# A fused mixer and mixture-of-experts layer in float32: the modulation's products move to VectorE, the first row norm is reordered, and eight unread products go

## What is computed

```python
def first_block(x, ...):
    hn = rmsnorm(x, norm_g)                       # the first row norm
    z = jnp.einsum('bsd,de->bse', hn, w_in)       # 1024 x 4252 weights, then split
    # attention in a band of chunks, an mLSTM and a gated linear attention (GLA) read pieces of z
    y = jnp.concatenate([y_a, y_b, y_c], axis=-1)
    return rmsnorm(x + jnp.einsum('bse,ed->bsd', y, w_out), final_g)

def second_block(x, c, ...):
    c_act = jax.nn.silu(c)
    mod = c_act @ ada_w[i] + ada_b[i]             # the modulation: 1024 x 6144 weights, one row
    sh1, sc1, gt1, sh2, sc2, gt2 = split(mod, 6)
    # a latent attention, an RWKV-7 recurrence, then 32 experts of width 1024, 4 for each token
```

## Time and profile before

| | |
|---|---|
| median of three runs | 1948.76 us |
| the profiled execution, its own time | 1948.07 us |
| its span in the trace | 1946.4 us |
| TensorE busy | 1865.2 us, 96% |
| VectorE busy | 1618.8 us, 83% |
| ScalarE busy | 1165.2 us, 60% |
| GpSimd busy | 366.1 us, 19% |
| TensorE's mean granted clock | 0.983 of full speed |

### The profile page before, as it was taken

The page is one execution under the profiler, slowest core; times in us unless marked ns, Lnnn a source line. Parts: engine busy times, 40 slices in busy tenths (PEclk is TensorE's granted clock), DMA queues, the critical chain, the costliest instruction groups (busy, mean ns, idle before and its releaser), DMA issues.

```text
span 1946.4 us, 27313 instructions
## 1 busy us (share of the span) xinstructions
PE 1865.2 (96%) x9416; PEld 1514.7 (78%) x9416; DVE 1618.8 (83%) x1719; ACT 1165.2 (60%) x1179; POOL 366.1 (19%) x356
## 2 busy tenths in 40 slices
PE   7999989999999888999999999999999999999997
PEld 6767767776677777888888888888888888888884
DVE  5776777954578487899999999999999999999996
ACT  5543344324462521577777777777777777777773
POOL 3431110020071710611101111111111111111110
PEclk9999999999998998999999999999999999999999
DMA  7535534232001143999999999999999999999994
GB/s 207 174 103 180 193 117 181 85 99 65 11 1 34 34 177 113 332 329 398 399 389 398 389 398 393 388 391 383 396 395 383 396 384 387 398 386 398 388 367 153
DMA packets 176818, 525.12 MB, mean 270 GB/s; under 512 B 30754, under 2 KB 48242, under 8 KB 176754
## 3 DMA queue, kind: packets, MB, share of 16 engines
q1 hardware_dynamic: 152722, 457.48, 61.8%
q0 software_dynamic: 21952, 66.78, 11.9%
q10 hardware_dynamic: 2080, 0.01, 0.1%
HBM read 499.08 MB, written 25.15 MB: 269 GB/s over the span
## 4 chain that ended last, share of the span: by engine, by line
PE 58%; DVE 2%; issue 0%; POOLq 0%; POOL 0%; DVEq 0%
PE banks L3625 54%; PE banks L3613 3%; PE banks L3619 1%; PE banks L3693 0%; DVE expert_weights L3973 0%; DVE x_tokens L3969 0%; DVE weights_lo L3764 0%; PE banks L3714 0%; DVE x_tokens L3980 0%; DVE x_tokens L3852 0%; PE banks L3751 0%; PE banks L3684 0%; DVE rows_lo L3794 0%; DVE member L3832 0%; DVE route_work L3874 0%
## 5 line engine op out<-in xcount | busy, mean ns | idle before, releaser
L3764 DVE TENSOR_TENSOR weights_lo<-expert_weights,weights_hi 128x2048 fp32r<-128x2048 f32 x384 | 876.0, 2288 | 66.0 <-ACT weights_hi L4011 62.8
L4011 ACT ACTIVATE weights_hi<-expert_weights 128x2048 fp32r<-128x2048 f32 x384 | 738.8, 1926 | 263.7 <-PE banks L3625 238.8
L3625 PE MATMUL banks<-weights_hi,rows_hi 128*128 128x512 f32 x1024 | 319.1, 393 | 0.0
L3625 PE MATMUL banks<-weights_hi,rows_lo 128*128 128x512 f32 x1024 | 315.5, 389 | 0.0
L3625 PE MATMUL banks<-weights_lo,rows_hi 128*128 128x512 f32 x1024 | 273.8, 389 | 0.0
L3625 PEld LDWEIGHTS banks<-weights_hi,rows_hi 128*128 128x128 f32 x1024 | 189.7, 188 | 44.9 <-issue 7.3
L3625 PEld LDWEIGHTS banks<-weights_hi,rows_lo 128*128 128x128 f32 x1024 | 192.2, 188 | 40.5
L3625 PEld LDWEIGHTS banks<-weights_lo,rows_hi 128*128 128x128 f32 x1024 | 192.2, 188 | 40.0
L3625 PE MATMUL banks<-weights_hi,u_hi 128*128 128x512 f32 x512 | 161.0, 396 | 0.0
L3625 PE MATMUL banks<-weights_hi,u_lo 128*128 128x512 f32 x512 | 157.9, 390 | 0.0
L3625 PE MATMUL banks<-weights_lo,u_hi 128*128 128x512 f32 x512 | 136.9, 389 | 0.0
(11 more groups left out here) (624 smaller groups left out, 2751.1 us busy)
## 6 DMA issues: line engine op xcount, KB each, us to landing
expert_weights<-in_exp_w SPq DMA_DIRECT2D x384, 1024.0 KB, 10.5
enter_rows<-in_ada_w POOLq DMA_DIRECT2D x24, 1024.0 KB, 6.9
w_in_landing<-in_w_in SPq DMA_DIRECT2D x16, 384.0 KB, 3.4
second_landing<-in_w_in SPq DMA_DIRECT2D x12, 512.0 KB, 3.7
x_tokens<-in_x SPq DMA_DIRECT2D x8, 512.0 KB, 7.1
w_in_landing<-in_w_in SPq DMA_DIRECT2D x8, 512.0 KB, 3.7
rwkv_room<-in_w_o SPq DMA_DIRECT2D x8, 512.0 KB, 7.8
w_in_landing<-in_w_in SPq DMA_DIRECT2D x12, 256.0 KB, 4.1
```

Source lines behind the costliest of these rows:

```text
L3625: last = nc.tensor.matmul(c.banks[:, bank + n, :], left[:, 2 * q + kk, :], right[:, q, kk * FF + n * 512:kk * FF + (n + 1) * 512], start=s ...
L3764: nc.vector.tensor_tensor(w_lo[:, ch % SPLIT, :], c.raw[:, ch % RAW if place is None else place, :], w_hi[:, ch % SPLIT, :], ALU.subtract) ...
L4011: nc.scalar.activation(w_hi[:, ch % SPLIT, :], c.raw[:, ch % RAW if place is None else place, :], ACT.Copy).then_inc(hi_ready.sem, 1)
```

## The change

It does five things.

1. `LATE` goes: `add_part` on VectorE does the products and sums of all 24 halves. `scale_half` (ScalarE) and `add_half` (GpSimd) go, eight calls of each. The 32 new operations of VectorE stand at `m` = 6 to 9, 14 to 17, 22 to 25, 30 to 33, 37 to 40, 47 to 50, 54 to 57 and 62 to 65. None stands at 41 to 46.
2. `load_half(i)` waits for VectorE's part of half `i - 2` instead of GpSimd's.
3. The first load of the modulation's weights waits until the last tile of `x` has landed.
4. The row norm: VectorE squares tile 2 before it inverts tile 1's root, and tile 3 before tile 2's. The last tile is normalised by VectorE instead of ScalarE. TensorE starts piece 0 with two low feature parts ready instead of four, and waits for the third and fourth ahead of its banks 2 and 3.
5. The eight unread products ahead of the first sum go.

```diff
-    LATE = 8
+    gate_chain = range(gates_at + 9, gates_at + 15)
     part_at, at_m = {}, 0
     for m, i in sorted(half_at.items()):
-        for kk in range(4 if i >= LATE else 0):
-            at_m = max(at_m + 1, m)
+        for kk in range(4):
+            at_m = max(at_m + 1, m - 1 if i == 4 else m)
+            if at_m in gate_chain:
+                at_m = gate_chain.stop
             part_at[at_m] = (i, kk)
...
-                    if i >= LATE + 2:
-                        pool.wait_ge(part_added.sem, 4 * (i - 1 - LATE))
-                    elif i >= 2:
-                        pool.wait_ge(half_added.sem, i - 1)
+                    if i >= 2:
+                        pool.wait_ge(part_added.sem, 4 * (i - 1))
...
+                pool.wait_ge(x_in[TT - 1].sem, 16)
                 load_half(0)
...
-                        pe.wait_ge(hn_lo.sem, max(2 * q + 2, TT if q == 0 else 0))
+                        pe.wait_ge(hn_lo.sem, 2 * q + 2)
+                    if g == 0 and q == 0 and b >= 2:
+                        pe.wait_ge(hn_lo.sem, b + 1)
...
                 def add_partitions(q):
                     own_last_bank(row_done, q + 1)
-                    if q == 0:
-                        idle(c.banks[:, 7, :], 8)
-                    if 2 * q < LATE:
-                        pe.wait_ge(half_added.sem, 2 * q + 2)
-                    else:
-                        pe.wait_ge(part_added.sem, 4 * (2 * q + 2 - LATE))
+                    pe.wait_ge(part_added.sem, 4 * (2 * q + 2))
...
-                for t in range(TT):
+                def root(t):
                     act.wait_ge(squares.sem, t + 1)
                     nc.scalar.activation(stat[:, 1, t:t + 1], stat[:, 0, t:t + 1], ACT.Sqrt).then_inc(roots.sem, 1)
+                root(0)
+                for t in range(TT - 1):
+                    if t >= 1:
+                        root(t + 1)
                     act.wait_ge(inverses.sem, t + 1)
                     nc.scalar.activation(y[:, t, :], c.x[:, t, :], ACT.Copy, scale=stat[:, 1, t:t + 1]).then_inc(normed.sem, 1)
+                    if t == 0:
+                        root(1)
...
+                square(0)
+                invert(0)
+                square(1)
+                for t in range(2, TT):
+                    square(t)
+                    invert(t - 1)
+                invert(TT - 1)
+                dve.wait_ge(inverses.sem, TT)
+                v.tensor_scalar(y[:, TT - 1, :], c.x[:, TT - 1, :], stat[:, 1, TT - 1:TT], None, ALU.mult).then_inc(last_normed.sem, 1)
                 low(0)
```

More of the change, by code:

```diff
@@ L673, in _ @@
                         mask_corner(i - 19)
-                    if i - 1 < LATE:
-                        add_half(i - 1)
                     if i % 2 == 0 and i >= 4:
@@ L954, in silu_last @@
                     nc.scalar.activation(tok_e[:, b, :], c.banks[:, b, :], ACT.Silu).then_inc(gates_made.sem, 1)
-                def scale_half(i):
-                    q, half = divmod(i, 2)
-                    act.wait_ge(w_in[half].sem, 16 * (q + 1))
-                    if i == 0:
-                        act.wait_ge(c_ready.sem, 1)
-                    for kk in range(4):
-                        k = 4 * half + kk
-                        last = nc.scalar.activation(w_m[:, half, kk, :], w_m[:, half, kk, :], ACT.Copy, scale=c_col[:, k:k + 1])
-                    last.then_inc(half_scaled.sem, 1)
                 def logs():
```

48 lines of the change are left out of this document (17 added, 31 removed).

## The result

The changed kernel took **1931.53 us** in the median of six runs (1928.59 to 1939.87) against 1950.18 us of the kernel before in the same series (six runs): a ratio of **0.9909 [0.9887, 0.9932]**. The forecast was 1943.0 us with a range of 1937 to 1951, so the time lies outside the range, and the move is three times the forecast one. The profiled execution of the changed kernel is the slowest of its six, 1939.87 us (span 1938.0 us), so its early stages are to be read, and not its end. The move of the medians, 18.7 us, is known to about 4 us by the interval.

The account below looks back on a forecast made before the run. TensorE, busy 96% of the span, was taken as the bound, with its waits and low clock. The terms -2.8 + 1.7 - 2.7 - 3.0 + 2.0 - 1.0 gave -5.8 us: 1943.0 us against the median, range 1937 to 1951.

Parts of the forecast that it names:

- the first sum: Mixers' first modulation sum: starts at 47.0 us behind VectorE's eighth operation instead of 49.79, -2.8 us.
- a fall of the clock behind it: Behind the first sum: TensorE idle about 3 us, then 3.4 us at half rate, +1.7 us (0 to +3.0).
- first sum to columns: Ahead of the turned gate columns: VectorE's chain ends earlier and TensorE's wait goes, -2.7 us.
- low clock behind the columns: Behind the turned gate columns: the low clock goes with the wait, -3.0 us (0 if the chain is not shortened).
- the third sum: At m = 51: a new wait for VectorE's half 5 operations, +2.0 us, between 0 and +3.5.
- the GLA's wait and the one at L755: In the GLA: the 1.0 us wait behind slow VectorE operations goes, -1.0 us, between -1.0 and +1.
- the row norm: At the start: piece 0 begins 1.3 to 1.9 us earlier, but spent at the first sum; 0, otherwise 3.6.
- The low part of piece 4: Ahead of the first sum: without GpSimd it ends near 35.3 us instead of 36.50, 1.2 us earlier.
- rival A: At the first sum: the clock does not fall, 1.7 us not paid; 1941.3 us, or 1939; chance 0.30.
- speak against this change: First sum: the skill's clock gate text taken as a sign that removing unread products lets the clock fall.
- VectorE's load: Between 30 and 142 us: 23.8 us added at most, some 15 us back from slow operations, about 9 us net.
- rival D: Later clock falls, as near 253 us, may come or go, 1.7 to 3 us either way; no chance given.

Follow-up runs that it names:

- e3: The kernel before with VectorE making products and sums of all 24 halves; old norm, early load and eight unread products stay: 1938.42 us, ratio 0.9959.
- e1: The changed kernel with the modulation's first load early again, not waiting for the last tile of x: 1936.27 us, ratio 0.9945.
- e2: The changed kernel with the old row norm order and piece 0 waiting for four low parts: 1931.90 us, ratio 0.9932.
- e7: The kernel before without the eight unread products ahead of the first sum: 1947.07 us, ratio 0.9994.
- e8: The kernel before with the new order of the row norm alone: 1947.17 us, ratio 0.9994.
- e5: The changed kernel with the eight unread products put back ahead of the first sum: 1940.43 us, ratio 0.9943.
- e6: The changed kernel without the 11, 4 and 7 unread products ahead of gate columns, keys and first GLA scores: 1932.84 us, ratio 0.9929.
- e11: The changed kernel with 76 more unread products at the head of the latent attention, shifting later stages back: 1949.73 us, ratio 1.0005.
- e9: The changed kernel itself run once more, with nothing changed: 1932.46 us, ratio 0.9916.
- e4: The kernel before with only the modulation's first load waiting for the last tile of x: 1948.69 us, ratio 1.0015.
- e10: The changed kernel without the 4 and 7 unread products ahead of keys and GLA scores, the columns' 11 kept: 1932.09 us, ratio 0.9913.
- e12: The changed kernel with VectorE's modulation operations allowed inside the gate chain, quarters 41 to 46: 1931.02 us, ratio 0.9911.

## Why the prediction was wrong

The prediction's terms beside the trace, up to the end of the mixers (us):

| step | predicted | measured |
|---|---|---|
| the first sum | -2.8 | -5.8 |
| a fall of the clock behind it | +1.7 | 0 |
| first sum to columns | -2.7 | -4.8 |
| low clock behind the columns | -3.0 | -3.1 |
| the third sum | +2.0 | +0.6 |
| the GLA's wait and the one at L755 | -1.0 | -1.6 |
| behind the GLA | not counted | -2.3 |
| sum | -5.8 | -16.9 |

The fourth to sixth rows split the window from the columns to the GLA (-4.0 us) by its busy time and its waits, within 0.1 us.

**The step that failed** is "It starts when VectorE has done its eighth operation ... The sum starts at 47.0 instead of 49.79 ... TensorE ... is idle for about 3 us ahead of it", and with it the row norm's "both are spent at the first sum, where something else is last; the term is 0". The low part of piece 4 was sized well: forecast to end at 35.3, measured 34.98 with the VectorE part alone (e3). From there the prediction took the 9.0 us that the load of piece 6 had needed before; it needed at most 7.6 us (35.0 to 42.58), and why it was shorter stays open. The eighth operation ended at 45.2. That is 1.2 us ahead of TensorE even with the old start. The late load and the norm together brought the same operation to 43.54 (45.72 without the late load in e1, 46.40 without the norm in e2). TensorE stayed last, and three things that the prediction had weighed against one another paid together: the start with its clock (-2.5: 1.0 of start, 1.5 of clock), the eight products (-2.0) and the wait (-1.3). They make the 5.8. These 4.7 us at the first sum and behind it are the largest part of the 11.1 us between forecast and trace. An estimate over a chain of five links was used as if it were good to 1 us; between "VectorE last by 3 us" and "TensorE last by 0.4 us" lay those 4.7 us, and rival A was written as a smaller gap, not as no gap at all.

**The fall behind the first sum** was priced rightly and placed wrongly. e7 and e8 show it in the kernel before, where the gap is 3.18 us and 2.19 us. The Trainium skill says in "TensorE: Matmul & The Clock Gate", Part 1, that the throttled state is the default and that activity releases it; the low clock behind the two gaps agrees. It did not speak against this change, since there was no idle time left for the unread products to fill (e5).

**The gate columns** came out as forecast: the wait gone, the clock 1.00, the low clock's 3.0 us measured as 3.1. The chain was even earlier than the 90 to 93 us given for L1185, which ended at 84.2. Two more waits stood on the way to the columns and were not in the sum: 0.94 us at L733 and 0.48 us at the second sum at 75.39. They went too, in e3 as well, where VectorE's part is the only change. With them the stretch from the first sum to the columns gave 4.8 us instead of 2.7.

**VectorE's load.** The estimate was that some 15 us of slow operations come back and the load rises by 9 us. It rose by 2.1. By the durations of the changed kernel the new operations cost 4 x 0.48 + 28 x 0.75 = 22.9 us, so 21 us came back. The cause given, GpSimd's additions, is borne out: with them gone the longest low part is 1.23 us (3.42 before) and the median stays. ScalarE's multiplications went in the same edit and could be the cause instead; the two traces settle it. Of VectorE's operations in the mixers that both kernels have, 15 were more than 0.1 us slower before, by 19.5 us together. Each of the 15 ran beside an addition of GpSimd; none of the 20 that ran beside a multiplication of ScalarE alone is among them. The Trainium skill ("SBUF — State Buffer", SBUF: two separate sides) says that an operation of VectorE with two SBUF inputs and one of GpSimd that reads SBUF exclude each other for their whole length; the trace agrees, with 5.44 us for two low parts beside a 2.65 us addition of GpSimd, and 1.22 and 1.01 us without.

**The third sum.** The wait came, but 0.6 us long and not 2.0: the whole chain ahead of it had moved with VectorE's shorter operations. Taking TensorE's products away shows it at full size, 3.11 us (e6).

**Behind the GLA** the prediction left the fall near 253 us to rival D, "each is worth 1.7 to 3 us either way". That was right: the same program shows it in e11 and not in e9. Of the profiles of the kernel before with one part changed, it is there in e7 and e8 and not in e3 and e4; of those of the changed kernel, in e2, e10 and e11 and not in the others. About 1.7 of the 16.9 us is therefore luck of the profiled executions. The start has luck in it too, the other way: its low clock in the kernel before was 3.4 us in this profile and 6.8 us in e7, and with the longer one the lead would be 1.1 us larger.

**Device time.** In the medians the changed kernel spends 52 and 58 us at 1.2 GHz and the kernel before 70 to 74; beside one another on one chip it is 58 against 74 (e9), 16 us less, worth 8. The waits, the eight products and the shorter chain make the rest, 6 to 8 us (net 1905.7 and 1905.8 against 1911.9 to 1914.0). The falls in the mixers' profile are 13.6 us, and 10.2 of these are placed by the program (the start and the columns), though their length varies from 3.4 to 6.8 us. What makes the late low clock near 610, 680 and 760 us longer in one execution than in another stays open; it goes with a spread of 4 to 17 us between the runs of one kernel and hid every difference of a few us between e1, e2, e5, e6, e10 and e12.

## What to carry to other kernels

- Before a gain is written off as absorbed, compare the two arrivals at that wait with an error on each. Where they lie within 2 to 3 us of one another, both cases belong in the forecast, and the sum of all upstream gains is one of them.
- When the engine that slows a neighbour is taken out of a stretch, many waits in the stretch can shrink, as here, and with them the low clock behind each. Count them all; the price of a wait is its length plus what the clock loses behind it.
- Unread products pay only in front of idle time. Look for the next wait before taking them out (e6), and try each part of a change with the others (e2 and e8).

## What was unexpected in the hardware

- A low clock of 3.4 us or more followed the waits of 2.19 us (e8), 2.28 (e1), 2.71 (before), 3.11 (e6), 3.18 (e7) and 3.84 us (before), and none followed 1.31 us at 49.79 in the kernel before, 1.6 us at the start of e6, e10 and e12, or 1.8 us ahead of the keys in e4. In between it is not fixed: after the 1.9 us near 236 us the same program fell in one execution and not in another (e11, e9).
- Its length is not fixed either: behind the same wait of 3.84 us at the start it is 3.4 us in the kernel before and 6.8 us in e7, which is the same program up to there. That alone moved the first sum by 1.1 us.
- One small load on SyncE's queue (the gates' bias) held the queue 11.49 us (e1), and 6.59 us in the changed kernel, where the modulation's first 2 MB come later. Everything queued behind it, piece 2 among it, moved by 5.1 us.
- The runs of one kernel differ by 4 to 17 us (12 runs of e3: 1929.72 to 1946.55 us, with 46 to 82 us at 1.2 GHz). The changed kernel's landmarks repeat within 0.1 us up to 312 us where no low clock falls in between (after, e9), so a difference of 2 us can be read there and not in the device time; where the low clock differs it has to be taken off first (before and e7: 1.1 us, e9 and e11: 1.7 us at 312 us).
